# Second rows of x requested after the first weights; last rows' product by column halves

## What is computed

```python
h = x                                    # 256 x 1024, f32
for block in (retention, mlp, conv, mlp, gla, mlp, retention, mlp):
    h = h + rmsnorm(block(rmsnorm(h, g1)), g2)
for block in (diff_attention, mlp, dilated_attention, mlp):
    h = h + block(rmsnorm(h, g))
# mlp(u) = square(relu(u @ w_up)) @ w_down,  w_up 1024 x 4096, w_down 4096 x 1024
# retention(u): u @ w_in, w_in 1024 x 6144, then the heads, then @ w_out
return h
```

## Time and profile before

| | |
|---|---|
| median of three runs | 2264.96 us (2263.76 to 2265.09) |
| the profiled execution's own time | 2263.4 us |
| its span in the trace | 2261.5 us |
| granted TensorE clock, mean | 0.988 |
| TensorE matmul busy | 2206.3 us, 98% of the span |
| VectorE, ScalarE, GpSimd busy | 66%, 53%, 10% |
| DMA | 368.93 MB, mean 163 GB/s |

### The profile page before, as it was taken

How to read it: one execution, slowest core, us unless ns; L and a number is a source line. 1 busy time by engine, 2 the same in 40 slices (tenths; PEclk the granted TensorE clock), 3 DMA queues, 4 the chain that set the end, 5 groups by cost and what they waited for, 6 DMA issues and landing times.

```text
span 2261.5 us, 29454 instructions
## 1 busy us (share of the span) xinstructions
PE 2206.3 (98%) x11632; PEld 1867.2 (83%) x11632; DVE 1482.9 (66%) x2070; ACT 1204.9 (53%) x1828; POOL 223.7 (10%) x204
## 2 busy tenths in 40 slices
PE   7999999999999999999999999988999999999999
PEld 7878888988888878889778888767888888798887
DVE  6645755897556667657636666886665898465655
ACT  5555544756445655455555444656445565455443
POOL 0000000662000020000001000001000000162000
PEclk9999999999999999999999999989999999899999
DMA  7534656615555436555544755523655766302653
GB/s 256 186 130 149 200 191 193 176 44 160 194 192 177 146 98 210 193 194 177 168 149 155 209 188 186 170 91 107 205 186 168 204 173 187 112 1 94 194 194 115
DMA packets 201528, 368.93 MB, mean 163 GB/s; under 512 B 6943, under 2 KB 142495, under 8 KB 201392
## 3 DMA queue, kind: packets, MB, share of 16 engines
q1 hardware_dynamic: 197776, 358.70, 48.8%
q0 software_dynamic: 3616, 8.35, 2.1%
HBM read 365.97 MB, written 1.05 MB: 162 GB/s over the span
## 4 chain that ended last, share of the span: by engine, by line
PE 91%; DVE 4%; ACT 2%; POOL 1%; issue 1%; DMA 0%; DVEq 0%; SPq 0%; ACTq 0%
PE PS L666 47%; PE PS L787 14%; PE PS L784 6%; PE PS L771 6%; PE PS L822 2%; PE PS L981 2%; PE PS L1327 2%; PE PS L1296 1%; PE PS L902 1%; DVE wlo L1953 1%; PE PS L829 1%; PE PS L1072 1%; PE PS L786 1%; POOL wlo L2836 1%; PE PS L1311 1%
## 5 line engine op out<-in xcount | busy, mean ns | idle before, releaser
L1953 DVE TENSOR_TENSOR wlo<-raw,whi 128x1024 fp32r<-128x1024 f32 x658 | 791.4, 1229 | 190.2 <-ACT whi L1382 189.4
L1382 ACT ACTIVATE whi<-raw 128x1024 fp32r<-128x1024 f32 x680 | 699.6, 1054 | 376.9 <-PE PS L666 312.7
L666 PE MATMUL PS<-whi,U 128*128 128x512 f32 x1728 | 486.9, 398 | 7.6 <-DVE U L2722 1.5
L787 PE MATMUL PS<-U,whi 128*128 128x512 f32 x1344 | 474.4, 397 | 0.0
L666 PEld LDWEIGHTS PS<-whi,U 128*128 128x128 f32 x1728 | 324.5, 190 | 81.7 <-issue 13.7
L784 PE MATMUL PS<-U,wlo 128*128 128x256 f32 x1176 | 330.0, 281 | 0.0
L787 PEld LDWEIGHTS PS<-U,whi 128*128 128x128 f32 x1344 | 247.0, 188 | 48.5
L666 PE MATMUL PS<-wlo,U 128*128 128x512 f32 x864 | 269.3, 393 | 0.0
L2072 DVE TENSOR_TENSOR AR<-PS,AR 128x512 f32<-128x512 f32 x96 | 66.3, 691 | 309.3 <-ACT AR L1468 309.3
L666 PE MATMUL PS<-whi,fH 128*128 128x512 f32 x832 | 258.2, 392 | 0.9 <-DVE fL L2210 0.9
L666 PE MATMUL PS<-whi,fL 128*128 128x512 f32 x832 | 256.3, 389 | 0.0
(11 more groups left out here) (326 smaller groups left out, 2413.4 us busy)
## 6 DMA issues: line engine op xcount, KB each, us to landing
raw<-in_mlp_w_up SPq DMA_DIRECT2D x64, 1024.0 KB, 5.5
raw<-in_mlp_w_down SPq DMA_DIRECT2D x64, 1024.0 KB, 5.0
raw<-in_ret_w_in SPq DMA_DIRECT2D x48, 1024.0 KB, 5.3
raw<-in_m_w_up SPq DMA_DIRECT2D x32, 1024.0 KB, 5.6
raw<-in_m_w_down SPq DMA_DIRECT2D x32, 1024.0 KB, 5.0
raw<-in_kv_w SPq DMA_DIRECT2D x24, 1024.0 KB, 5.3
raw<-in_ret_w_out SPq DMA_DIRECT2D x16, 1024.0 KB, 4.9
raw<-in_gla_w_in SPq DMA_DIRECT2D x12, 1024.0 KB, 5.2
```

What stands on the lines that cost most here:

```text
L666: mm = e.matmul(bank(b + nb), a, w[:, nb * 512:(nb + 1) * 512], start=(begins and n < 2), stop=(ends and n >= 4))
L787: mm = e.matmul(o, w_h[:, k, :], U[:, k, :, :, :], start=(k == 0), stop=(k == 7))
L1382: e.activation(split_half(whi, i, x), raw_halves(i)[x], ACT.Copy).then_inc(HI.tick((i, x)), 1)
L1953: e.tensor_tensor(split_half(wlo, i, x), a, split_half(whi, i, x).bitcast(F32), ALU.subtract).then_inc(LO.tick((i, x)), 1)
```

## The change

Three edits in one diff. SP asks for x of tt = 1 only after chunk 0 has landed, directly ahead of chunk 1. In the last MLP the second row tile of the last product is computed column half by column half: all twelve matmuls into bank 2, then all twelve into bank 3, with a semaphore increment ("left") after the first twelve. VectorE's addition of the left half waits for that increment alone, and SP stores each column half by itself: four stores of 256 KB in place of two of 512 KB.

```diff
@@ gemms
+        gemms.append((LAST, "left"))
@@ gemm_last
-                for tt in range(2):
+                for tt in range(2 if S != LAST else 1):
@@
+                if S == LAST:
+                    for nb in range(2):
+                        n = slice(nb * 512, nb * 512 + 512)
+                        for k in range(4):
+                            i, k2 = i0 + k // 2, k % 2
+                            w_h, w_l = split_half(whi, i, k2), split_half(wlo, i, k2)
+                            a_h, a_l = ap(k, 1)
+                            e.matmul(bank(2 + nb), a_h, w_h[:, n], start=False, stop=False)
+                            e.matmul(bank(2 + nb), a_h, w_l[:, n], start=False, stop=False)
+                            mm = e.matmul(bank(2 + nb), a_l, w_h[:, n], start=False, stop=(k == 3))
+                            if nb == 1:
+                                mm.then_inc(USED.tick((i, k2)), 1)
+                        if nb == 0:
+                            mm.then_inc(TOP.tick((S, "left")), 1)
@@ add_plain
-                e.wait_ge(*rows_done((S, "y"), tt))
                 for j in range(2):
+                    e.wait_ge(*(TOP[S, "left"] if (S, tt, j) == (LAST, 1, 0) else rows_done((S, "y"), tt)))
@@ sp_program
             load_chunk(0)
-            load_x(1)
-
             e.wait_ge(*landed(0))
+            load_x(1)
             for i in range(1, NCH):
                 load_chunk(i)
             for tt in range(2):
                 for j in range(2):
                     e.wait_ge(*HN[LAST + 1, tt, j])
-                e.dma_start(out[0, tt * 128:tt * 128 + 128, :], h[:, tt, :]).then_inc(s_out, 16)
-            e.wait_ge(s_out, 32)
+                    c = slice(512 * j, 512 * j + 512)
+                    e.dma_start(out[0, tt * 128:tt * 128 + 128, c], h[:, tt, c]).then_inc(s_out, 16)
+            e.wait_ge(s_out, 64)
```

More of the change, by code:

```diff
@@ L2997, in sp_program @@
             load_chunk(0)
+            e.wait_ge(*landed(0))
             load_x(1)
-            e.wait_ge(*landed(0))
             for i in range(1, NCH):
```

## The result

The changed kernel takes 2268.02 us (median of 22 runs, 2265.49 to 2269.64), the kernel before, measured beside it, 2264.77 (22 runs, 2261.01 to 2265.69). The ratio is 1.0017, with a 95% interval of 1.0011 to 1.0023, or 2.5 to 5.2 us; the medians by themselves differ by 3.25 us. It is slower, clear of zero, and the 3.25 us lie inside the 0.2% (4.5 us) that was called no change. Forecast were +4.0 us and a median of 2269.0.

What follows compares the result with a forecast made beforehand. TensorE, busy 98% of the span, was taken as the bound, so head and tail changes carry to the end. Head +3.2 (with -0.2 in it), clock +2.1 and tail -1.3 gave +4.0 us, median 2269.0, range 2263.2 to 2270.8.

Steps and rivals of the forecast that it cites:

- Chunk 0 without x: Head: chunk 0 lands earlier without x of tt = 1 beside it, -0.2 us; bounds nothing and 2.0 us gain.
- The falling rate (319, then 250 GB/s): Head, chunk 0's load: 250 GB/s after 319 speaks against a full path, hence only -0.2 us.
- The sign of being wrong set down for this: Head: if chunk 0 lands by 9.4, then x was what held it.
- Chunk 1 behind x: Head: x goes ahead in chunk 1's queue, so chunk 1 lands at 20.0, some 9.5 us after request instead of 5.3.
- The byte count: Head: 0.60 MB of chunk 1 left at 14.5, moving at 0.115 MB/us beside POOL's tables; last byte at 19.7.
- The stall: Head: ScalarE waits for chunk 1, U of tt = 1 starts at 22.0 instead of 18.83, VectorE and TensorE follow; +3.2 us.
- The clock: Head: TensorE rests about 4 us, returns at half clock at 23.4; +2.1 us, between 1.5 and 2.9.
- The rival without a fall of the clock: Head: stall but no clock loss; +1.9 us in all, 2266.9; chance 0.12.
- The rival with the longest half clock: TensorE's return at 23.4: 6.7 us slow costs 2.9, chunk 1 later (+3.8); +5.4 in all, 2270.4; chance 0.19.
- The end: Tail: one addition after the last matmul (-0.66) and a halved last store (-0.65); -1.3 us, -0.6 to -1.5.
- The formula: Tail, last store: 2.0 us plus the bytes at 436 GB/s, an estimate of 0.6 us saved for the half.
- The sum: Whole kernel: +3.2 + 2.1 - 1.3 = +4.0 us; profiled execution 2267.4, median 2269.0; chance 0.48.

Runs made afterwards that it cites:

- ScalarE's order alone: Against the kernel before: on ScalarE, U of tt = 1 goes ahead of chunk 1's high part; 2264.00 against 2264.23 us, ratio 0.9997.
- the order exchanged: Against the changed kernel: SP asks for chunk 1 ahead of x of tt = 1; 2262.43 us, 0.9990 against the kernel before.
- POOL's tables later: Against the changed kernel: POOL asks for c_rel and norm_gains after chunk 1 has landed, not chunk 0; 2262.19 us, 0.9989 against the kernel before.
- head alone: Against the kernel before: only x of tt = 1 asked for after chunk 0 has landed, end unchanged; 2269.37 against 2264.74 us, ratio 1.0024.
- the filled rest: Against the changed kernel: 18 unread matmuls added on TensorE behind the transposes of tt = 1; 2266.43 us against 2264.54 of the kernel before, 1.0009.
- the three executions with the small tables moved: Against the kernel before: POOL's three small tables asked for after chunk 0, twice; once with x of tt = 1 moved too; 2269.20, 2269.82 and 2268.86 us.
- the end alone: Against the changed kernel: load of x of tt = 1 put back where it was; 2263.30 us against 2264.74 of the kernel before, 0.9993.
- ScalarE's order: Against the changed kernel: on ScalarE, U of tt = 1 goes ahead of chunk 1's high part; 2261.86 us against 2264.54 before, 0.9989.

## Why the prediction was right

**Chunk 0 without x.** This term was mis-sized. Forecast was -0.2 us, with bounds 0 and 2.0; in the profile it was -1.8, and over all traces -1.55. The step that failed is "its tail was a few DMA engines that had fallen behind ... Taking x away helps a straggler only as far as the shared path was the limit". The runs showed in its place that x counts for 1.55 us as long as POOL's small tables are there too, which the prediction left out. How they hinder chunk 0 stays open. The falling rate (319, then 250 GB/s) that I took as a sign of a free path was none: with chunk 0 latest of all (9.4 us, ScalarE's order alone) the same two windows show 273 and 292 GB/s. The sign of being wrong set down for this, chunk 0 landing by 9.4, came: it landed at 8.56.

**Chunk 1 behind x.** Forecast to need some 9.5 us after its request in place of 5.3, and to land at 20.0; it needed 10.6 and landed at 19.54. The byte count carried over because q1's share did not change: 0.74 MB in six microseconds against 0.69. The runs with the order exchanged (5.2 us) and with POOL's tables later (6.1) show both parts of the cause. The Trainium skill's rule of turns between the queues, packet by packet ("DMA: Bandwidth & Descriptors", section Queues, rings and completion order), would have left q1 a fifth, if each packet that the profile counts were one turn; with 735 packets to 406 it is not one to one, as it was not before. By the same section a packet can hold several descriptors, so the counts don't refute the rule itself, only that way of working with it.

**The stall.** +3.2 forecast for the return of TensorE; +2.6 in the profile (22.87 against 20.25), +3.4 in the trace with the head alone (23.66). Chunk 0, and so the request of chunk 1, came 1.6 us earlier than assumed, and chunk 1 took 1.1 us longer from its own request. Two errors cancelled here in part: the term came out right to within the spread for a reason that is half luck.

**The clock.** +2.1 forecast, between 1.5 and 2.9. Profile: 4.06 - 2.62 = 1.4, with 3.3 us at half clock; head alone: 6.0 - 3.4 = 2.6, with 5.9 us; the filled rest gives back 1.4. The three executions with the small tables moved rested too, 4.09, 5.45 and 4.32 us, and paid 1.4, 2.1 and 1.5 us, taken as what they needed from TensorE's return to chunk 1's run beyond the 4.11 of before. The forecast lies inside what single executions show, 1.4 to 2.6. The rival without a fall of the clock is refuted by all five traces. The rival with the longest half clock (6.7 at the head) is what the trace of the head alone comes near to (30.38, +6.0), but not what the medians do.

**The end.** -1.3 forecast, -1.3 in the profile (3.2 against 4.5 us), -1.4 in the medians of the end alone. Writing one bank twelve times in a row cost nothing: the chain has 0.23 us per matmul there as before. The formula that the prediction took from the Trainium skill ("DMA: Bandwidth & Descriptors", section Anatomy of one DMA) is given there for transfers issued by GpSimd. Worked out from it, estimates for 256 and 512 KB are 2.6 and 3.2 us; SP's stores took 2.0 and 2.6, so only the difference of 0.6 agrees.

**The sum.** Profile: +4.06 - 1.3 = +2.8, while the spans differ by 4.1. The other 1.3 us came about between 28 and 2257 us, in stages the change doesn't touch; in the stretch of 1480 to 1560 us the granted clock was 0.83 before and 0.77 after. One execution each can't say that the change is behind that, and the medians, +4.6 and -1.4 for its two parts and +3.25 for both, give no sign of it. So it is luck that the profiled execution took just the 2267.4 us forecast for it: the two ends give 1.2 us less than the +4.0 of the sum. The median lies 0.6 us above it, not the 1.56 of the kernel before.

## What to carry to other kernels

Moving a transfer out of the way of the one that is awaited moves it into the way of the next. Count, in bytes and for each queue, what has to pass before every landing behind it, and look in the order of the consuming engine for work that stands behind that landing without needing it: here half a megabyte more at the wrong moment became 4.6 us of stall and lost clock, net of what chunk 0 gained, and exchanging two requests, or two calls on ScalarE, turned +3.25 into -2.3 to -2.7. At the end of a kernel, split the last product by output columns, so that only one part's addition and store come after the last matmul (1.3 us here).

## What the runs showed of the hardware

- Beside a load of 512 KB in its own queue and three small loads in the software queue, a load of 1 MB landed 8.3 to 9.4 us after its request (3 traces); beside the small ones alone in 6.9 to 7.7 (8), beside the 512 KB alone in 7.3 and 6.7 (2), beside neither in 6.5 (1).
- With runs of 4 KB asked for by POOL in q0 and runs of 1 KB in q1, q0 moved two thirds of the bytes: 1.51 MB to 0.69 in six microseconds before, 1.47 to 0.74 after.
- Rests of TensorE of 4.09, 4.32, 4.61, 4.82 and 5.45 us were followed by 3.4, 3.4, 3.3, 5.9 and 4.8 us at the 1.2 GHz level; rests of 0.80 us by none. The prices were 1.4, 1.5, 1.4, 2.6 and 2.1 us. Behind the first rest, ahead of chunk 0, the slow stretch was 2.7 us (POOL's tables later) to 5.7 us (ScalarE's order): one event, no fixed price.
- 17 unread matmuls ahead of the first real ones brought these to 0.12 us from the second on, and 18 in a rest, which left 1.50 us of it idle, held the clock at its 2.4 GHz level.
- Twelve matmuls of 512 columns in a row into one bank took 0.23 us each, as when they alternated between two banks. A store of 256 KB landed in 2.0 us where one of 512 KB took 2.6.
